# Expert weights read as contiguous row groups, with the rows they meet in a permuted column order

## The chip, the cores and the metric

The kernel runs on one core of a Trainium2 chip. The metric is device time in microseconds (us) of one execution, lower is better. The core has a matrix engine (TensorE, PE in the profile, with its weight loads as PEld), a vector engine (VectorE, DVE), a scalar engine (ScalarE, ACT), GpSimd (POOL) and SyncE (SP), which issues most of the transfers (DMA) from HBM, the memory of the chip, to SBUF, the memory beside the engines. PSUM is the memory that matmuls write, in eight banks.

## The reference, cut to what matters

One layer of an encoder for two groups of tokens (256 prompt tokens and 64 sample tokens, 320 in all). After retention, attention and a first layer norm, its last part is a mixture of 32 experts, of which each token uses two:

```python
h = x * (1 + sc2) + sh2                              # 320 x 1024
logits = h @ w_rg + b_rg, h @ w_re + b_re            # router: 4 groups, 32 experts
# for each expert e, the tokens t that chose it, with gate g:
a, u = jnp.split(h[t] @ w_e_in[e], 2, axis=-1)       # w_e_in[e]: 1024 x 1024
y    = ((jax.nn.silu(a) * u) @ w_e_out[e]) * g       # w_e_out[e]: 512 x 1024
x = layer_norm(alpha * x + (1 + g2) * y_moe)
```

All is in float32. A sum over the 1024 columns of `h` (or the 512 of `silu(a) * u`) may be taken in any order, as long as the rows of the weight go in the same order.

## The kernel before, in words

The instructions of each engine are written out by hand, in one program for each engine, with semaphores between them. Every weight passes through the same stream in pieces of 1 MB (128 partitions x 2048 float32): SyncE loads a piece into one of six buffers `w_raw`; ScalarE rounds it to the reduced float format of fast matmuls (`w_hi`, three buffers, L816 and L973); VectorE takes the difference `w_lo = w_raw - w_hi` (L1061, L1566); TensorE multiplies by both. So the product keeps nearly full precision.

The dense part of the layer takes the first 680 us or so. Then `h2`, the input of the experts, is made on VectorE for three tiles of up to 128 tokens (L1417, L1419, L1421), turned by TensorE (L1925) and copied to `h2T` (L961) for the router (L1914), and written to HBM (L726, L728). VectorE works out from the router's logits which tokens each expert has. An *item* is one expert with up to 64 of its tokens; in this input there are 32 items.

For item e, GpSimd gathers the rows of `h2` from HBM into `x_item` (L741), TensorE turns them in eight blocks of 128 columns (L1957), and ScalarE and VectorE split them (L978, L1570) into `xT_item`. The six pieces of an item in the stream are four of `w_e_in` (j = 0 to 3, two blocks of 128 rows each) and two of `w_e_out` of the item before (j = 4 and 5). Pieces 0 to 4 are split into `w_hi` and `w_lo`; piece 5 is multiplied as it is, at full precision (L1976). The hidden row `silu(a) * u` of 512 columns is made on VectorE by `hidden` (L1579), turned in four blocks by TensorE (L1983), split (L990, L1583) and met with `w_e_out`. The item's result is added up on VectorE (L1590) and scattered to HBM by GpSimd (L747, L774).

The order of one turn of the loop over the items, which is what the prediction follows:

```python
# VectorE, turn e                        # ScalarE, turn e
item_lo(e, 0)                            item_hi(e, 0)
hidden(e - 1)          # L1579           silu(e - 1)
item_lo(e, 1)                            item_hi(e, 1)
y_sum(e - 2, third)                      y_low(e - 2, ...)
item_lo(e, 2)                            item_hi(e, 2)
hidden_low(e - 1)                        hidden_high(e - 1)
item_lo(e, 3); item_lo(e, 4)             item_hi(e, 3); item_hi(e, 4)
au_sum(e); x_low(e + 1)                  au_low(sub(e, 3)); x_high(e + 1)
```

TensorE, turn e: products of pieces 0 and 1 (for each, four matmuls with `w_hi`, L1964, and four with `w_lo`, L1968), the turning of the hidden rows of item e - 1 (L1983), products of pieces 2 and 3, the turning of the input rows of item e + 1 (L1957), the product of piece 4, and that of piece 5 (L1976). SyncE issues piece j of the next item when `w_lo` j has been made (for piece 5, when its product is done), in the order j = 0 to 5 (L532).

Of the kernel before, what the change touches and what calls it, by code (L numbers as in the profile page):

```python
# [13 lines left out]
ALU = mybir.AluOpType  # L14
# [7 lines left out]
P = 128  # L22
KD = D // P
RH, DK, DV = 4, 128, 256
FH, DH = 16, 64
NG, EG, NE = 4, 8, 32
# [77 lines left out]
def build_layer(nc, i, o, scratch):  # L104
# [26 lines left out]
    def at(name, shape, dt, offset):  # L131
        size = int(np.prod(shape[1:])) * (2 if dt == BF16 else 4)
        assert PH + offset + size <= END, (name, PH, offset, size)
        return nc.alloc_sbuf_tensor_at(name, shape, dt, offset=PH + offset)
# [81 lines left out]
    g1x = at("affine_tmp", [P, D], F32, 16384)  # L216
# [4 lines left out]
    def rt(name, shape, dt=F32):  # L221
        t = at(name, shape, dt, ro["n"])
        ro["n"] += (int(np.prod(shape[1:])) * (2 if dt == BF16 else 4) + 31) // 32 * 32
        assert ro["n"] <= 32768
        return t

    wr = rt("w_router", [P, KD, NG + NE])
# [54 lines left out]
    auS = at("au_sum", [SLOTS, 2, FE], F32, 12288)  # L282
    aA = at("a_silu", [SLOTS, FE], F32, 16384)
    hid = at("hidden", [SLOTS, FE], F32, 18432)
# [13 lines left out]
    def sem(name):  # L298
        return ctx.enter_context(nc.semaphore(name))
# [23 lines left out]
    res_in, ln_in, ln_var, ln_std, h2_ready, h2_out, h2T_done = (  # L323
        sem(n) for n in ("res_in", "ln_in", "ln_var", "ln_std", "h2_ready", "h2_out", "h2T_done"))
    m2_in, m2_ready, wr_in, r_dve, r_act, msk_done, slots_ready, slt_done, idx_ready = (
        sem(n) for n in ("m2_in", "m2_ready", "wr_in", "r_dve", "r_act", "mask_done",
                         "slots_ready", "slt_done", "idx_ready"))
    nb_ready, xn_ready = sem("shift_ready"), sem("normalised")
    row_cp, x_norm, x1_ready, nit_ready = sem("row_copied"), sem("x_normalised"), sem("x1_ready"), sem("items_counted")
    idx_cp, x_landed, x_trans, x_hi, x_split, au_lo, au_drained, silu_ok, hid_ok = (  # L330
        sem(n) for n in ("idx_copied", "x_landed", "x_transposed", "x_hi", "x_split", "au_low_copied",
                         "au_drained", "silu_done", "hidden_done"))
# [48 lines left out]
    def spare(after):  # L381

        return tuple(dense_banks(CI[after] + 1)) + (6, 7)
# [23 lines left out]
    for h in range(RH):  # L407
        s = spare("ga0")
# [42 lines left out]
    def bcast(ap1d, rows):  # L451

        return ap1d.partition_broadcast(rows)

    w_in_e = i["w_e_in"][0].rearrange("e (k p) n -> e p k n", p=P)
    w_out_e = i["w_e_out"][0].rearrange("e (k p) n -> e p k n", p=P)
    E0 = N0 + 4
    assert E0 % NRAW == 0 and E0 % NSPL == 0
    PLAIN = 5
# [108 lines left out]
    def _(pool):  # L568
        st = Steps(pool, own_pool)
# [56 lines left out]
        for t in range(3):  # L626
            rows = P if t < 2 else DEC
# [23 lines left out]
        for t in range(3):  # L651
            rows = P if t < 2 else DEC
            st(nc.gpsimd.tensor_scalar(qaug[0:rows, t, :, DH], f_tok[0:rows, q_slots[t], :], 8.0, None, ALU.mult))
        for t in range(4):
            rows = P if t < 3 else DEC
# [60 lines left out]
            st.settle()  # L716

        pool.wait_ge(evacuated, CI["wo0"] + 1)
        pool.dma_start(wr[:, :, 0:NG], i["w_rg"][0].rearrange("(k p) n -> p k n", p=P)).then_inc(wr_in, 16)
        pool.dma_start(wr[:, :, NG:], i["w_re"][0].rearrange("(k p) n -> p k n", p=P)).then_inc(wr_in, 16)  # L720
        pool.dma_start(br[:, 0:NG], bcast(i["b_rg"][0], P)).then_inc(wr_in, 16)
        pool.dma_start(br[:, NG:], bcast(i["b_re"][0], P)).then_inc(wr_in, 16)

# [64 lines left out]
        for t in range(3):  # L788
            rows = P if t < 2 else DEC
# [18 lines left out]
    def _(act):  # L808
# [13 lines left out]
        def copy_bank(key, dst, src):  # L822

            b, _, f, d = use[key]
            act.wait_ge(*f)
            st(nc.scalar.activation(dst, src(b), ACT.Copy), d)
# [8 lines left out]
        def split_hi(kind, dst):  # L835
            for k in range(KD):
                b, _, f, _ = use[(kind, k)]
                act.wait_ge(*f)
                st(nc.scalar.activation(dst[:, k, 0:T], b[:, 0:T], ACT.Copy), ts_hi)

        act.wait_ge(c_in, 32)
        st(nc.scalar.activation(cs2[:], c2[:], ACT.Silu), c_silu)
        b, _, f, _ = use["cT"]
        act.wait_ge(*f)
        act.wait_ge(fills_done, 1)
# [208 lines left out]
    def _(dve):  # L1054
        st = Steps(dve, own_dve)
        V = nc.vector
# [226 lines left out]
        for t in range(3):  # L1283
            rows = P if t < 2 else DEC
# [4 lines left out]
        for t in range(3):  # L1289
            rows = P if t < 2 else DEC  # L1290
# [11 lines left out]
        for t in range(3):  # L1302
            rows = P if t < 2 else DEC
# [9 lines left out]
        for w_, op in ((gnw, ALU.mult), (gnb, ALU.add)):  # L1313
            st.settle()
            for t in range(3):
                rows = P if t < 2 else DEC
# [3 lines left out]
        for t in range(3):  # L1320
            rows = P if t < 2 else DEC
# [91 lines left out]
        for t in range(3):  # L1413
            rows = P if t < 2 else DEC
            xt, ht = x1[0:rows, t, :], h2[0:rows, t, :]
            m2 = m2p if t < 2 else m2s
            st(V.tensor_scalar(xt, xt, mv[0:rows, t, 0:1], mv[0:rows, t, 1:2], ALU.subtract, ALU.mult), x_norm)  # L1417
            st.settle()
            st(V.tensor_tensor(ht, xt, m2[0:rows, 1, :], ALU.mult))  # L1419
            st.settle()  # L1420
            st(V.tensor_tensor(ht, ht, m2[0:rows, 0, :], ALU.add), h2_ready)  # L1421


        iota = const("iota")
# [151 lines left out]

        def hidden(e):
            dve.wait_ge(silu_ok, e + 1)
            V.tensor_tensor(hid[:], aA[:], auS[:, 1, :], ALU.mult).then_inc(hid_ok, 1)  # L1579

        def hidden_low(e):
            dve.wait_ge(hh_hi, e + 1)
# [14 lines left out]
        def item_steps(e, second, third):  # L1597
            item_lo(e, 0)
            hidden(e - 1)
            item_lo(e, 1)  # L1600
            if second:
                y_sum(e - 2, third)
            item_lo(e, 2)
            hidden_low(e - 1)
            item_lo(e, 3)
            item_lo(e, 4)
            au_sum(e)
            x_low(e + 1)
# [4 lines left out]
        with dve.Fori(3, n_items) as e:  # L1613
            item_steps(e, True, True)
        item_lo(n_items, 0)
        hidden(n_items - 1)
        item_lo(n_items, 1)
        y_sum(n_items - 2, True)
# [426 lines left out]
```

## Time and profile before

| what | value |
|---|---|
| median of 3 runs | 1299.65 us (1297.51 to 1302.85) |
| the profiled execution | 1297.03 us, span from first to last instruction 1295.2 us |
| TensorE busy | 1104.2 us, 85% |
| VectorE busy | 894.2 us, 69% |
| ScalarE busy | 634.2 us, 49% |
| HBM read | 299.97 MB |
| expert loads | 128 pieces of `w_e_in` and 64 of `w_e_out`, 1 MB each |

The busy shares are averages over stages that differ. The loop over the items runs from about 725 us to 1245 us of the span, 40% of it; in it all of TensorE, VectorE and the transfer engines are marked busy for nine tenths of the time or more.

### The profile page before, as it was taken

To read this page: it belongs to the slowest core of one execution; us is meant where nothing else is said; L and a number is where in the kernel's file an instruction comes from. 1 tells how busy PE (TensorE), PEld (TensorE's weight loads), DVE (VectorE), ACT (ScalarE), POOL (GpSimd) and SP (SyncE) were. 2 spreads that over 40 slices of the span, in tenths; PEclk is the share of its full clock that TensorE was granted. 3 is DMA by queue.
4 is the path that set the end of the run, shared out by engine and by line. 5 is a ranking of instruction groups with operands and counts; after the bars stand their busy time and mean duration, and the time that the engine had idled before them with its cause. 6 is when DMAs were issued, how large, how long until landed. Compare 5 with 4: busy or idle time off the path is not lost.

```text
span 1295.2 us, 13399 instructions
## 1 busy us (share of the span) xinstructions
PE 1104.2 (85%) x4460; PEld 761.4 (59%) x4460; DVE 894.2 (69%) x974; ACT 634.2 (49%) x639; POOL 267.6 (21%) x227
## 2 busy tenths in 40 slices
PE   5798899888899999999854799999999999999960
PEld 2365568566687666678644556666666666666640
DVE  3868843367464333345596699999999999999957
ACT  3654232222322222332221477777777777777732
POOL 0331940010001000000460741111111111111210
PEclk8798989988999555589785699999999999999985
DMA  9767243153725500024623589999999999999933
GB/s 321 253 238 257 94 152 130 48 169 104 272 73 137 205 0 0 0 98 162 213 68 109 190 336 389 389 393 393 395 395 393 397 391 396 394 390 400 397 110 116
DMA packets 102661, 303.33 MB, mean 234 GB/s; under 512 B 10740, under 2 KB 10788, under 8 KB 102118
## 3 DMA queue, kind: packets, MB, share of 16 engines
q1 hardware_dynamic: 92888, 282.75, 58.6%
q0 software_dynamic: 9744, 20.19, 5.2%
q8 instruction: 18, 0.29, 0.1%
q14 instruction: 11, 0.09, 0.0%
HBM read 299.97 MB, written 14.73 MB: 243 GB/s over the span
## 4 chain that ended last, share of the span: by engine, by line
PE 59%; DVE 18%; DMA 7%; ACT 7%; issue 5%; POOL 4%; SPq 0%; ACTq 0%; POOLq 0%; DVEq 0%
PE banks L1968 9%; PE banks L1976 7%; PE banks L1964 7%; PE banks L1694 6%; PE banks L1700 6%; DVE w_lo L1566 6%; ACT w_hi L973 5%; PE banks L1696 4%; DMA w_raw<-in_w_in 3%; DVE w_lo L1061 3%; PE banks L1727 2%; PE banks L1957 2%; ACT w_hi L816 2%; PE banks L1983 1%; DMA w_raw<-in_w_ada 1%
## 5 line engine op out<-in xcount | busy, mean ns | idle before, releaser
L1566 DVE TENSOR_TENSOR w_lo<-w_raw,w_hi 128x2048 fp32r<-128x2048 f32 x157 | 361.3, 2318 | 36.8 <-ACT w_hi L973 36.8
L973 ACT ACTIVATE w_hi<-w_raw 128x2048 fp32r<-128x2048 f32 x157 | 295.5, 1903 | 0.2 <-issue 0.2
L1061 DVE TENSOR_TENSOR w_lo<-w_raw,w_hi 128x2048 fp32r<-128x2048 f32 x72 | 173.2, 2423 | 137.8 <-ACT w_hi L816 137.7
L816 ACT ACTIVATE w_hi<-w_raw 128x2048 fp32r<-128x2048 f32 x72 | 136.5, 1910 | 210.5 <-PE banks L1700 94.7
L1968 PE MATMUL banks<-w_lo,xT_item 128*128 128x512 f32 x512 | 150.5, 416 | 45.2 <-DVE w_lo L1566 45.2
L1964 PE MATMUL banks<-w_hi,xT_item 128*128 128x512 f32 x512 | 158.9, 433 | 4.2 <-ACT w_hi L973 2.8
L1694 PE MATMUL banks<-w_hi,h_hi 128*128 128x512 f32 x384 | 142.2, 411 | 13.1 <-ACT w_hi L816 12.6
L1968 PEld LDWEIGHTS banks<-w_lo,xT_item 128*128 128x128 f32 x512 | 93.5, 193 | 91.3 <-DVE w_lo L1566 73.1
L1964 PEld LDWEIGHTS banks<-w_hi,xT_item 128*128 128x128 f32 x512 | 96.0, 193 | 39.1 <-issue 14.3
L1976 PE MATMUL banks<-w_raw,hiddenT 128*128 128x512 f32 x248 | 111.4, 592 | 0.0
L1700 PE MATMUL banks<-w_lo,h_hi 128*128 128x512 f32 x384 | 108.2, 404 | 2.4 <-DVE w_lo L1061 2.4
L747 POOL DMA_INDIRECT scratch_y<-y_item,slot_row x29 | 62.8, 2166 | 229.2 <-DVE y_item L1590 212.5
L1696 PE MATMUL banks<-w_hi,h_lo 128*128 128x512 f32 x256 | 105.2, 411 | 0.0
L1694 PEld LDWEIGHTS banks<-w_hi,h_hi 128*128 128x128 f32 x384 | 75.1, 196 | 34.0 <-ACT w_hi L816 14.9
L1700 PEld LDWEIGHTS banks<-w_lo,h_hi 128*128 128x128 f32 x384 | 73.6, 193 | 22.3 <-DVE w_lo L1061 4.6
L1976 PEld LDWEIGHTS banks<-w_raw,hiddenT 128*128 128x128 f32 x248 | 47.0, 189 | 47.3 <-issue 44.5
L741 POOL DMA_INDIRECT x_item<-scratch_h,slot_token x32 | 32.3, 1009 | 183.1 <-PE banks L1957 153.9
L994 ACT ACTIVATE au_low<-banks 64x1024 f32<-64x1024 f32 x32 | 32.8, 1024 | 62.2 <-PE banks L1968 62.2
L1696 PEld LDWEIGHTS banks<-w_hi,h_lo 128*128 128x128 f32 x256 | 50.9, 199 | 11.9
L1717 PE MATMUL banks<-w_lo,c_parts 128*64 128x512 f32 x96 | 34.1, 488 | 15.6 <-DVE w_lo L1061 15.2
L986 ACT ACTIVATE y_low<-banks 64x1024 f32<-64x1024 f32 x32 | 32.8, 1024 | 26.4 <-PE banks L1976 17.3
L1575 DVE TENSOR_TENSOR au_sum<-banks,au_low 64x1024 f32<-64x1024 f32 x32 | 38.9, 1216 | 7.7 <-ACT au_low L994 5.2
(438 smaller groups left out, 1579.3 us busy)
## 6 DMA issues: line engine op xcount, KB each, us to landing
w_raw<-in_w_e_in SPq DMA_DIRECT2D x128, 1024.0 KB, 7.3
w_raw<-in_w_e_out SPq DMA_DIRECT2D x64, 1024.0 KB, 6.0
w_raw<-in_w_in SPq DMA_DIRECT2D x32, 1024.0 KB, 9.0
w_raw<-in_w_ada SPq DMA_DIRECT2D x24, 1024.0 KB, 7.2
bias_rows<-in_b_in SPq DMA_DIRECT2D x16, 256.0 KB, 4.8
w_raw<-in_w_ret_proj SPq DMA_DIRECT2D x4, 1024.0 KB, 17.2
w_raw<-in_w_fox_proj SPq DMA_DIRECT2D x4, 1024.0 KB, 18.8
w_raw<-in_w_o SPq DMA_DIRECT2D x4, 1024.0 KB, 5.1
```

Of the source, the lines that this page charges most:

```text
L747: nc.gpsimd.indirect_dma_start(yd[:, :], bass.IndirectOffsetOnAxis(ap=row[:, e:e + 1], axis=0), ySb[:].rearrange("p a b -> p (a b)"), None ...
L816: nc.scalar.activation(whi[n % NSPL][:], raw[n % NRAW][:], ACT.Copy).then_inc(hi_done, 1)
L973: nc.scalar.activation(whi[ss][:], raw[j][:], ACT.Copy).then_inc(hi_done, 1)
L1061: V.tensor_tensor(wlo[n % NSPL][:], raw[n % NRAW][:], whi[n % NSPL][:].bitcast(F32), ALU.subtract).then_inc(lo_done, 1)
L1566: V.tensor_tensor(wlo[ss][:], raw[j][:], whi[ss][:].bitcast(F32), ALU.subtract).then_inc(lo_done, 1)
L1575: V.tensor_tensor(auS[:], banks[0:SLOTS, 0:2, :], auLo[:], ALU.add).then_inc(au_drained, 1)
L1694: mm(b[:, :], H[:, k, cols], whi[n % NSPL][:, kk, :], start=(k == 0), stop=False)
L1696: mm(b[:, :], L[:, k, cols], whi[n % NSPL][:, kk, :], start=False, stop=False)
L1700: last = mm(b[:, :], H[:, 4 * s + kk, cols], wlo[n % NSPL][:, kk, :], start=False, stop=(s == 1 and kk == 3))
L1964: mm(bank[b0 + half], X[:, k0 + kk, :], whi[ss][:, 2 * kk + half, :], start=(first and kk == 0), stop=False)
L1968: last = mm(bank[b0 + half], X[:, k0 + kk, :], wlo[ss][:, 2 * kk + half, :], start=False, stop=(final and kk == 1))
L1976: last = mm(bank[b0 + half], X[:, k0 + kk, :].bitcast(F32), raw[rs][:, 2 * kk + half, :], start=False, stop=(kk == 1))
```

## The change

`w_e_in`, `w_e_out` and the two router weights are read with another order of their rows. Before, partition p of block k held row 128 k + p, so that a piece of two blocks took two separate runs of 4 KB for each partition. After, partition p of block k holds row 8 p + k (for `w_e_out`, 4 p + k), so that a piece of two blocks is one run of 8 KB for each partition. The columns of `h2` and of the hidden row are put into the same order when they are written: position 128 k + p holds column 8 p + k (4 p + k). The last VectorE operation of `h2` and the operation `hidden` do that by reading their inputs with a stride: 8 elements (32 bytes) in `h2`, 4 elements (16 bytes) in `hidden`; both write neighbouring elements. The first product of `h2` goes to the buffer `affine_tmp` instead of `h2`, since the second can't permute in place. All turnings on TensorE read 128 neighbouring columns, as they did.

```diff
-    w_in_e = i["w_e_in"][0].rearrange("e (k p) n -> e p k n", p=P)
-    w_out_e = i["w_e_out"][0].rearrange("e (k p) n -> e p k n", p=P)
+    w_in_e = i["w_e_in"][0].rearrange("e (p k) n -> e p k n", p=P)
+    w_out_e = i["w_e_out"][0].rearrange("e (p k) n -> e p k n", p=P)
...
-        pool.dma_start(wr[:, :, 0:NG], i["w_rg"][0].rearrange("(k p) n -> p k n", p=P)).then_inc(wr_in, 16)
-        pool.dma_start(wr[:, :, NG:], i["w_re"][0].rearrange("(k p) n -> p k n", p=P)).then_inc(wr_in, 16)
+        pool.dma_start(wr[:, :, 0:NG], i["w_rg"][0].rearrange("(p k) n -> p k n", p=P)).then_inc(wr_in, 16)
+        pool.dma_start(wr[:, :, NG:], i["w_re"][0].rearrange("(p k) n -> p k n", p=P)).then_inc(wr_in, 16)
...
-            st(V.tensor_tensor(ht, xt, m2[0:rows, 1, :], ALU.mult))
-            st.settle()
-            st(V.tensor_tensor(ht, ht, m2[0:rows, 0, :], ALU.add), h2_ready)
+            st(V.tensor_tensor(g1x[0:rows, :], xt, m2[0:rows, 1, :], ALU.mult))
+            st.settle()
+            st(V.tensor_tensor(ht.rearrange("r (k p) -> r k p", k=KD), g1x[0:rows, :].rearrange("r (p k) -> r k p", k=KD),
+                               m2[0:rows, 0, :].rearrange("r (p k) -> r k p", k=KD), ALU.add), h2_ready)
...
-            V.tensor_tensor(hid[:], aA[:], auS[:, 1, :], ALU.mult).then_inc(hid_ok, 1)
+            V.tensor_tensor(hid[:].rearrange("s (k p) -> s k p", k=4), aA[:].rearrange("s (p k) -> s k p", k=4),
+                            auS[:, 1, :].rearrange("s (p k) -> s k p", k=4), ALU.mult).then_inc(hid_ok, 1)
```

## Rows read from the trace of the kernel before

**Rows 1.** One turn by windows: us; PE, PEld, DVE, ACT, POOL; clock, transfer share, GB/s.

```profile
913.57:929.95 16.38, 15.02 (x63) 9.92 (x63) 15.07 (x11) 12.55 (x11) 2.96 (x2) 1.00 1.02 395
```

**Rows 2.** Transfers from 760 to 1200 us: one queue, then issues by line.

```profile
q1 hardware_dynamic: 43807, 168.88, 98.7%
...
w_raw<-in_w_e_in SPq DMA_DIRECT2D x107, 1024.0 KB, 7.3
```

**Rows 3.** Waits from 760 to 1200 us: total us, times, longest.

```profile
PEld banks L1968 <- DVE w_lo L1566: 58.9, 53, 1.5
...
DVE w_lo L1566 <- ACT w_hi L973: 31.3, 54, 0.6
```

**Rows 4.** Waits of SyncE's queue, 700 to 1200 us.

```profile
SPq L532 <- DVE w_lo L1566: 232.3, 114, 8.6
SPq L532 <- PE banks L1976: 131.8, 28, 4.7
```

**Rows 5.** The tile w_raw from 760 to 1200 us: time from issue to landing.

```profile
DMA to landing us min/median/max: 4.8/7.3/9.1
```

**Rows 6.** Timeline of one turn: start, duration, instruction, idle before.

```profile
914.22 2.29 DVE L1566 TENSOR_TENSOR w_lo<-w_raw,w_hi 128x2048 fp32r<-128x2048 f32 x1 [0.61 <-ACT w_hi L973]
...
916.43 0.68 DVE L1579 TENSOR_TENSOR hidden<-a_silu,au_sum 64x512 f32<-64x512 f32 x1
...
917.03 2.28 DVE L1566 TENSOR_TENSOR w_lo<-w_raw,w_hi 128x2048 fp32r<-128x2048 f32 x1
...
918.09 8.27 SPq L532 DMA_DIRECT2D w_raw<-in_w_e_in  x4
...
919.40 0.89 PEld L1968 LDWEIGHTS banks<-w_lo,xT_item 128*128 128x128 f32 x4
...
925.88 0.77 PEld L1968 LDWEIGHTS banks<-w_lo,xT_item 128*128 128x128 f32 x4 [1.50 <-DVE w_lo L1566]
...
928.66 1.91 ACT L973 ACTIVATE w_hi<-w_raw 128x2048 fp32r<-128x2048 f32 x1
```

**Rows 7.** The chain that ended last, one turn: start, us, what.

```profile
937.11 0.56 PE banks L1983 x5
...
937.97 1.92 ACT w_hi L973
...
939.91 2.30 DVE w_lo L1566
...
942.26 1.20 PE banks L1968 x4
```

**Rows 8.** VectorE groups by shape, 600 to 735 us: busy, mean ns.

```profile
L1419 DVE TENSOR_TENSOR h<-x,mod_prompt 128x1024 f32<-128x1024 f32 x2 | 2.4, 1224 | 0.1
...
L1505 DVE TENSOR_REDUCE choice_pos<-onehot_tmp 128x6 f32<-128x192 f32 x1 | 0.4, 353 | 0.0
...
L1456 DVE TENSOR_REDUCE expert_logits<-expert_masked 128x24 f32<-128x96 f32 x1 | 0.3, 316 | 0.0
...
L1496 DVE TENSOR_REDUCE extra_items<-count_cmp 128x32 f32<-128x128 f32 x1 | 0.3, 286 | 0.0
```

**Rows 9.** Timeline where the third tile of h2 is turned.

```profile
680.42 1.22 DVE L1421 TENSOR_TENSOR h<-h,mod_sample 64x1024 f32<-64x1024 f32 x1
```

**Rows 10.** The chain that ended last, 670 to 735 us.

```profile
677.20 1.24 DVE h L1421
...
678.48 1.97 PE banks L1925 x8
...
683.71 1.04 PE banks L1925 x8
...
730.07 2.78 DVE hidden L1579
```

**Rows 11.** Page, groups: an operation that every item has once.

```profile
L1575 DVE TENSOR_TENSOR au_sum<-banks,au_low 64x1024 f32<-64x1024 f32 x32 | 38.9, 1216 | 7.7 <-ACT au_low L994 5.2
```

**Rows 12.** Transfer rate in 40 slices of 0 to 100 us (2 KB runs).

```profile
GB/s 14 299 324 388 421 245 288 386 388 385 388 387 244 352 406 114 389 383 317 381 281 206 213 0 38 228 281 368 401 360 395 320 227 203 217 22 2 14 297 362
```

## The prediction

> **What bounds the kernel now.** The change touches the item loop and the `h2` step ahead of it, so I read those stages alone. First the windows: one turn of the loop takes 16.38 us, and in it TensorE is busy 15.02 us, VectorE 15.07 us and the transfer engines all the time, at 395 GB/s [rows 1]. Three candidates look full, and the transfers look fullest: their queue holds the engines for 98.7% of the stretch from 760 to 1200 us [rows 2]. If they set the pace, longer runs might pay.
>
> So next the waits, which tell who is late. In that stretch TensorE waits for `w_lo` and VectorE for `w_hi` [rows 3]; no line of that view has an engine waiting for `w_raw`. The queue waits instead: in 700 to 1200 us SyncE stood 232.3 us for `w_lo` and 131.8 us for the product of piece 5, that is for a buffer to come free [rows 4]. A transfer lands 7.3 us after issue, at most 9.1 [rows 5]. How much time has it? Piece 0 is issued at 918.09 and ScalarE wants it at 928.66 [rows 6]: 10.6 us. The transfers are busy, but early by 1.5 us at worst and 3.3 us at the median. They don't set the pace.
>
> What does is read from the chain that ended last [rows 7]: turning of the hidden rows, `w_hi` of piece 3, `w_lo` of piece 3, its product. Ahead of the turning stand only products of TensorE. But the timeline shows a second cycle of the same length beside it [rows 6]. VectorE does `w_lo` 0 at 914.22, `hidden` at 916.43, `w_lo` 1 at 917.03 without a gap, and ends that at 919.31; TensorE loads its first weights for the product of `w_lo` 1 at 919.40. That is 0.09 us later, and where TensorE surely waited for `w_lo` (the 1.50 us ahead of 925.88 [rows 6]) the chain shows 0.04 to 0.05 us from the end of `w_lo` to the load: 2.30 us from 939.91 ends at 942.21, the product is at 942.26 [rows 7]. So `w_lo` 1 comes with at most 0.05 us to spare. Whatever delays it delays the turning, then `w_hi` 3, `w_lo` 3, the product, `au_low`, `w_hi` 0 and the next `w_lo` 0: a closed cycle.
>
> **The change part by part.**
>
> *Longer runs.* They are worth nothing while transfers aren't waited for. In the first 100 us, with runs of 2 KB, the queue sustained 385 to 388 GB/s in a row of slices [rows 12], with 4 KB runs 395 [rows 1]: even the rate seems to depend little on the run. I take 0. What hides it is the 1.5 to 3.3 us above. The cost if the new addresses are slower instead: 6 pieces of 1.05 MB make 6.29 MB in 16.38 us, or 384 GB/s for the weights alone; below about that rate the loop waits for them.
>
> *Router weights.* Two small GpSimd loads, of the same pieces of 16 and 128 bytes at the destination, so I take the same cost: nothing, as no engine waits for them in the chain [rows 10].
>
> *First product into `affine_tmp`.* It is the same shape, 1.224 us [rows 8], and GpSimd's last use of that buffer is waited for already: 0.
>
> *Strided reads.* This is the part that costs. No `tensor_tensor` of the trace reads with such a stride, but one reduction does: L1456 reads 96 elements, each 32 bytes from the one before within its group of four. It took 316 ns. Reductions with neighbouring elements took 353 ns for 192 elements and 286 ns for 128 [rows 8], so 1.05 ns an element over a base of 152 ns; 96 elements should take 253 ns. The stride cost 63 ns, 0.66 ns for each element.
>
> The bounds from this: below, 0 (if those 63 ns are peculiar to the reduction). The row's rate gives `hidden` 512 x 0.66 = 0.34 us. If an element takes two cycles instead of one, which a short row may not show in full, the extra is one more 1.05 ns: 0.54 us. If each of the two strided inputs pays at the row's rate, 0.68 us. I take the middle of the row's rate and the doubling, 0.44 us, so `hidden` 0.68 to 1.12 us: the row is the only one near, but it is short and has one input, where these have two, so I lean up from it. For `h2`, 1024 elements: 0.68, 1.07, 1.35 us; I take 0.87.
>
> The Trainium skill has a rule that speaks against this change: Advanced Engine Details and Errata, SBUF Cachelines, says that SBUF is read by lines of 16 bytes and that an access pattern with another line for each access pays a penalty, with no figure. Both new strides (16 and 32 bytes) are of that kind, and the row agrees in sign.
>
> *What of it is on the path.* `hidden` is called once an item, 32 times [rows 11], right ahead of `w_lo` 1. Its extra less the 0.05 us to spare goes through the cycle each time; in the first turn `hidden` stands in the chain itself [rows 10], and at the end the last `y_item` stands behind it on VectorE. So 32 x (0.44 - 0.03) = 13.1 us, with 0.03 as a middle for what is spare. Queued behind `hidden` on VectorE are `w_lo` 1, `y_item`, `w_lo` 2 and the low half of `hiddenT`; all move by the same amount, and so do the transfers that wait for them. The transfers get more time, so they are still not late.
>
> `h2`: the second operation of tiles 0 and 1 is in the chain (1.24 us at 677.20, then TensorE's turning at 678.48 [rows 10]). The third tile is ready at 680.42 + 1.22 = 681.64 [rows 9], but TensorE turns it at 683.71 [rows 10], so its own extra 0.87 lies under those 2 us. 2 x 0.87 = 1.7 us.
>
> Sum: 13.1 + 1.7 = 14.8 us. The profiled execution, 1297.03 us, becomes 1311.9; it lies 2.6 us below the median of the runs, 1299.65. The forecast is for the median: **1314 us**.
>
> **The rivals.**
>
> *Strides are free.* The 63 ns belong to the reduction. Then `hidden` stays 0.68 us, nothing on the path changes, and the time is 1299.65 us, no change. For it: a single short row. Against it: the other reductions fit one line to the nanosecond or two, this one is 25% off. The Trainium skill has a rule that would give this: VectorE: DVE Perf Modes, Mode 1× (REGULAR), says that the base mode yields one result a cycle and names odd strides among what it takes. The trace does not bear it out where L1456 is concerned. Chance 0.2. To it I add the case that the loop has more give than I read, so that only part of `hidden` shows and the whole stays under 6.5 us: 0.03.
>
> *The transfers were the bound after all.* Both look full [rows 1, 2]. If longer runs sped them, the turn could shrink towards VectorE's 15.07 us of work: 31 turns x 1.3 = 40 us, down to 1259 us. It needs transfers that are waited for, and no such wait is there [rows 3]; it would begin to count only if the waits ascribed to `w_hi` were in truth waits for `w_raw`. Chance 0.04.
>
> *The new addresses are slower.* Partitions now start 32 KB apart in `w_e_in` and 16 KB in `w_e_out`, instead of 4 KB. The point from which it decides is a landing later than 10.6 us after issue, or a rate below 6.29 MB / 16.8 us = 374 GB/s. At 324 GB/s, a slice of [rows 12], a turn would take 19.4 us and the time would be 1299.65 + 31 x 3.0 = 1393 us. Nothing in the trace speaks for it. Chance 0.04.
>
> **How the numbers follow.** The forecast case (strides cost, the loop passes it on) has 0.69. Its own range runs from the row's rate, 32 x (0.34 - 0.05) + 1.4 = 10.7, so 1310 us, to both inputs paying, 32 x (0.68 - 0.01) + 2.7 = 24.1, so 1324 us. To leave out no more than 0.2 in all, the range must take in free strides too, with the scatter of runs: 1298 to 1325. What a measurement here can tell from no change is about 0.5%, 6.5 us. Faster is the second rival with a little for scatter, 0.05; the same is the first, 0.22; slower is the forecast and the last rival, 0.73.
>
> **What would show it.** In the profile after: `hidden` (L1579 before) at 1.0 to 1.2 us and never below 0.9; the second operation of `h2` at about 2.1 us, the first at 1.22 still; turns of the item loop of 16.8 us; waits of TensorE for `w_lo` 1 that were not there, with all other idle times as before; landing times no longer than 7.3 us; half as many packets for the experts if a packet is a run. It is wrong if `hidden` stays at 0.68 us, if the turn is longer while `hidden` isn't, if it is longer by less than `hidden` is, or if a wait for `w_raw` turns up.

## The result and the profile after

| | before | after |
|---|---|---|
| median | 1299.7 us (13 runs, 1297.51 to 1305.01) | 1307.59 us (13 runs, 1301.54 to 1310.71) |
| profiled execution | 1297.03 us | 1303.19 us |
| span | 1295.2 us | 1301.3 us |
| one turn of the item loop, median | 16.38 us | 16.60 us |
| `hidden`, median | 0.68 us | 1.07 us |

The changed kernel takes 1.0048 of the time before, with an interval of 1.0031 to 1.0065. That is 6.2 us (4.0 to 8.4), which is also the difference of the means of the runs; the medians lie 7.9 us apart. So it is slower, by about the 0.5% that the prediction called no change. The forecast was 1314 us, 14 us above the median before. The direction is right, the size is about half.

Everything behind the making of `h2` has moved down by one or two lines: `hidden` is now L1580, `w_lo` L1567, the products are L1966 (`w_hi`), L1970 (`w_lo`) and L1978 (plain), the turning of the hidden rows L1985.

The first row sums up `hidden`, which now reads with a stride: count, then the shortest, median and longest duration in ns, then the first and the last start.

```profile
L1580 DVE TENSOR_TENSOR hidden<-a_silu,au_sum x32: 1052/1068/3325, 727.5 to 1249.8; 64x512 f32<-64x512 f32 x32
```

And from the timeline of `h2`'s making:

```profile
671.08 2.00 DVE L1421 TENSOR_TENSOR h<-affine_tmp,mod_prompt 128x1024 f32<-128x1024 f32 x1
```

`hidden` took 0.68 us [rows 6] and takes 1.07; the other took 1.22 [rows 8] and takes 2.00. That is (1068 - 676) / 512 = 0.77 ns for each element at steps of 16 bytes, where 676 ns is the median of `hidden` in the runs with neighbouring reads, and (2000 - 1224) / 1024 = 0.76 ns at steps of 32 bytes. The short reduction from which the prediction took its rate gave 0.66 [rows 8]. By the rule of the Trainium skill (Advanced Engine Details and Errata, SBUF Cachelines) there is a penalty for a new line at each access; the trace agrees, and the price is the same for 16 and 32 bytes.

Next the windows, two turns of the loop after the change (columns as in [rows 1]):

```profile
914.95:931.53 16.58, 15.23 (x63) 9.85 (x63) 15.45 (x11) 12.54 (x11) 2.96 (x2) 1.00 0.98 388
931.53:948.15 16.62, 15.28 (x63) 9.87 (x63) 15.47 (x11) 12.57 (x11) 3.15 (x2) 1.00 1.01 396
```

The granted clock is 1.00 in both, so the higher of the two levels, as before. VectorE's work has grown by 0.39 us a turn (15.07 to 15.46), the turn by only 0.22 (16.38 to 16.60). Over 32 items 0.22 us make 7.0 us, which with 2 x 0.78 = 1.6 us for `h2` is 8.6. That is a little more than the ratio gives (4.0 to 8.4 us) and than the medians do.

The two profiled executions show it more sharply, though they lie only 6.2 us apart. First `h2`'s first product, after and before, and then `hidden` of the kernel before:

```profile
669.82 1.22 DVE L1419 TENSOR_TENSOR affine_tmp<-x,mod_prompt 128x1024 f32<-128x1024 f32 x1
```

```profile
672.70 1.22 DVE L1419 TENSOR_TENSOR h<-x,mod_prompt 128x1024 f32<-128x1024 f32 x1
...
L1579 DVE TENSOR_TENSOR hidden<-a_silu,au_sum x32: 675/677/2858, 730.0 to 1244.0; 64x512 f32<-64x512 f32 x32
```

The changed kernel comes to this product 2.9 us sooner, though nothing ahead of it differs but the order of the rows in two small router loads: single executions scatter by as much in their first half. From there to the last `hidden` it takes 1249.8 - 669.82 = 580.0 us, where it was 1244.0 - 672.70 = 571.3: 8.7 us more, as the account has it. (One turn of this execution, the first, is 20.4 us long in place of 16.4, with a granted clock of 0.92; but the loop also begins earlier, and the second product of a piece 5 stands at 765.55 us where it stood at 765.98.)

Where the other 0.17 us went is seen in the timeline of one turn:

```profile
917.80 1.07 DVE L1580 TENSOR_TENSOR hidden<-a_silu,au_sum 64x512 f32<-64x512 f32 x1
...
918.80 2.27 DVE L1567 TENSOR_TENSOR w_lo<-w_raw,w_hi 128x2048 fp32r<-128x2048 f32 x1
...
919.84 0.89 PEld L1966 LDWEIGHTS banks<-w_hi,xT_item 128*128 128x128 f32 x4
920.07 1.10 PE L1966 MATMUL banks<-w_hi,xT_item 128*128 128x512 f32 x4
...
921.12 0.76 PEld L1970 LDWEIGHTS banks<-w_lo,xT_item 128*128 128x128 f32 x4 [0.40 <-DVE w_lo L1567]
921.13 1.20 PE L1970 MATMUL banks<-w_lo,xT_item 128*128 128x512 f32 x4
...
922.25 0.48 PEld L1985 LDWEIGHTS banks<-pack,hidden 64*128 64x128 f32 x5 [0.37 <-issue]
922.25 0.62 PE L1985 MATMUL banks<-pack,hidden 64*128 64x64 f32 x5
```

The weight load for `w_lo` 1 now waits 0.40 us, as forecast in kind. But there is no idle time on the row of its matmuls. While nothing is late, the matmuls run 0.23 us behind their loads (919.84 and 920.07). When the load is late they run right with it (921.12 and 921.13). So the loads run ahead, and a late one first uses that up. Part of it is lost again, since the four matmuls then take 1.20 us in place of 1.10. From this load to the turning of the hidden rows it is now 1.13 us (921.12 to 922.25). The same stretch before, in the timeline of the kernel before:

```profile
919.63 1.10 PE L1968 MATMUL banks<-w_lo,xT_item 128*128 128x512 f32 x4
...
920.66 0.48 PEld L1983 LDWEIGHTS banks<-pack,hidden 64*128 64x128 f32 x5 [0.37 <-issue]
```

With the load at 919.40 [rows 6] it was 1.26 us. Now the account closes: `hidden` is 0.39 us longer, 0.04 us of that was to spare before the load (the prediction's step), 0.13 us are made up between load and turning, and 0.22 us are left.

No line of the waits from 760 to 1200 us has an engine waiting for `w_raw`; one that was not there before is TensorE's for `x_item`, once, 1.7 us. TensorE's waits for `w_lo` grew from 53 to 79 (of 27 turns, so one more a turn), 9.6 us in all:

```profile
PEld banks L1970 <- DVE w_lo L1567: 68.5, 79, 1.3
...
DVE w_lo L1567 <- ACT w_hi L973: 27.7, 54, 1.2
```

And the transfers of that stretch:

```profile
q1 hardware_dynamic: 22763, 165.78, 95.2%
...
w_raw<-in_w_e_in SPq DMA_DIRECT2D x105, 1024.0 KB, 6.9
```

About half as many packets, a share of 95.2% in place of 98.7%, and landing 6.9 us after issue in place of 7.3 [rows 2]. For each percent of the engines' time the queue moved 165.78 / 95.2 = 1.741 MB, against 168.88 / 98.7 = 1.711 before: 1.8% more. Longer runs do make the transfers cheaper, and nobody was waiting for them.

### The profile page after: what moved, and what is told of

It reads as the page before. It is cut to its first block, busy times and chain, and to the rows that moved or that the text cites. A ratio compares the mean times of both kernels' runs of the same rounds, so it can differ in the third digit from the quotient of the medians.

```text
span 1301.3 us, 13399 instructions
## 1 busy us (share of the span) xinstructions
PE 1105.5 (85%) x4460; PEld 756.1 (58%) x4460; DVE 906.7 (70%) x974; ACT 634.4 (49%) x639; POOL 277.5 (21%) x227
## 4 chain that ended last, share of the span: by engine, by line
PE 60%; DVE 14%; DMA 8%; POOL 7%; ACT 6%; issue 4%; SPq 1%; ACTq 0%; POOLq 0%; DVEq 0%
PE banks L1970 9%; PE banks L1978 7%; PE banks L1966 7%; PE banks L1696 7%; PE banks L1702 6%; DVE w_lo L1567 5%; PE banks L1698 4%; ACT w_hi L973 4%; DMA w_raw<-in_w_in 3%; DVE w_lo L1061 2%; PE banks L1959 2%; PE banks L1729 2%; ACT w_hi L816 1%; PE banks L1985 1%; DMA w_raw<-in_w_ada 1%
## 5 line engine op out<-in xcount | busy, mean ns | idle before, releaser
L1567 DVE TENSOR_TENSOR w_lo<-w_raw,w_hi 128x2048 fp32r<-128x2048 f32 x157 | 360.3, 2312 | 32.7 <-ACT w_hi L973 32.7
L973 ACT ACTIVATE w_hi<-w_raw 128x2048 fp32r<-128x2048 f32 x157 | 295.6, 1903 | 0.2 <-issue 0.2
L1970 PE MATMUL banks<-w_lo,xT_item 128*128 128x512 f32 x512 | 152.5, 420 | 45.6 <-DVE w_lo L1567 45.6
L1966 PE MATMUL banks<-w_hi,xT_item 128*128 128x512 f32 x512 | 159.1, 433 | 4.2 <-ACT w_hi L973 2.8
L1970 PEld LDWEIGHTS banks<-w_lo,xT_item 128*128 128x128 f32 x512 | 91.1, 192 | 100.6 <-DVE w_lo L1567 85.3
L1966 PEld LDWEIGHTS banks<-w_hi,xT_item 128*128 128x128 f32 x512 | 95.9, 193 | 39.0 <-issue 14.1
L1978 PE MATMUL banks<-w_raw,hiddenT 128*128 128x512 f32 x248 | 111.5, 592 | 0.0
L1978 PEld LDWEIGHTS banks<-w_raw,hiddenT 128*128 128x128 f32 x248 | 47.0, 190 | 47.2 <-issue 44.5
L741 POOL DMA_INDIRECT x_item<-scratch_h,slot_token x32 | 36.7, 1146 | 174.8 <-PE banks L1959 146.6
L994 ACT ACTIVATE au_low<-banks 64x1024 f32<-64x1024 f32 x32 | 32.8, 1024 | 60.1 <-PE banks L1970 60.1
L1592 DVE TENSOR_TENSOR y_item<-banks,y_low 64x1024 f32<-64x1024 f32 x32 | 38.8, 1213 | 8.0 <-ACT y_low L986 8.0
```

The source lines that it names most:

```text
L973: nc.scalar.activation(whi[ss][:], raw[j][:], ACT.Copy).then_inc(hi_done, 1)
L1567: V.tensor_tensor(wlo[ss][:], raw[j][:], whi[ss][:].bitcast(F32), ALU.subtract).then_inc(lo_done, 1)
L1592: V.tensor_tensor(ySb[:], banks[0:SLOTS, 2:4, :], yLo[:], ALU.add).then_inc(y_drained, 1)
L1966: mm(bank[b0 + half], X[:, k0 + kk, :], whi[ss][:, 2 * kk + half, :], start=(first and kk == 0), stop=False)
L1970: last = mm(bank[b0 + half], X[:, k0 + kk, :], wlo[ss][:, 2 * kk + half, :], start=False, stop=(final and kk == 1))
L1978: last = mm(bank[b0 + half], X[:, k0 + kk, :].bitcast(F32), raw[rs][:, 2 * kk + half, :], start=False, stop=(kk == 1))
```

## The experiments

Eleven kernels, each set against runs of the kernel before that were made with it. The turn is that of the profiled execution, the median of 30 turns between successive plain products of the item loop; single turns that are longer are named in the text. Where a part of the row order is left out, the text says so. For the three reordered kernels, whose turns vary, it is the mean of 28 turns between successive `hidden`, without the first two and the last.

| kernel | median us | ratio to before | turn us |
|---|---|---|---|
| runs alone | 1301.29 | 1.0015 [0.9998, 1.0031] | 16.38 |
| `hidden` alone | 1303.70 | 1.0038 [1.0023, 1.0053] | 16.60 |
| `h2` alone | 1302.44 | 1.0024 [1.0009, 1.0040] | 16.37 |
| after, `hidden` behind `w_lo` 1 | 1297.24 | 0.9986 [0.9972, 0.9999] | 16.37 |
| strided writes | 1303.18 | 1.0026 [1.0008, 1.0044] | 16.52 |
| strided turnings | 1335.12 | 1.0281 [1.0248, 1.0314] | 17.35 |
| 0.15 us more behind `hidden` | 1301.05, one run | | 16.37 |
| 0.38 us more behind `hidden` | 1304.54, one run | | 16.55 |
| after, loop reordered | 1283.53 | 0.9875 [0.9852, 0.9897] | 15.94 |
| before, loop reordered | 1290.27 | 0.9918 [0.9899, 0.9936] | 16.21 |
| runs alone, loop reordered | 1282.65 | 0.9859 [0.9837, 0.9881] | 15.90 |

### Longer runs alone

```diff
-    w_in_e = i["w_e_in"][0].rearrange("e (k p) n -> e p k n", p=P)
-    w_out_e = i["w_e_out"][0].rearrange("e (k p) n -> e p k n", p=P)
+    w_in_e = i["w_e_in"][0].rearrange("e (p k) n -> e p k n", p=P)
+    w_out_e = i["w_e_out"][0].rearrange("e (p k) n -> e p k n", p=P)
```

The permutation of `h2`, of the hidden row and of the router weights is left out; the work of each engine is that of before.

> The weights of the experts are read in 8 KB runs, but no column is permuted (the router's weights, h2 and hidden stay as before), so hidden rows and weight rows don't match: the kernel leaves the permutation out, and its work is otherwise that of the kernel before. Theory A (transfers are early, the loop is paced by the engines): turns of the item loop stay at 16.38 us, the time is that of before within 3 us, landing times about 6.9 us. Rival B (8 KB runs give something that the strided reads hid): turns under 16.3 us and a time 3 to 10 us below before. Rival C (the new addresses cost part of the loss): turns of 16.45 us or more, 2 to 7 us slower.

1301.29 us over 12 runs, ratio 1.0015 with an interval that holds 1. Turns of 16.38 us but for one of 17.89. `w_raw` landed at 4.9, 6.9 and 9.1 us (shortest, median, longest), where it was 4.8, 7.3 and 9.1 [rows 5]. So in the turns the longer runs bring nothing and the new addresses cost nothing. The loss isn't in the transfers.

### `hidden` alone, and `h2` alone

The first takes the new order for `w_e_out` and the strided `hidden`; the second takes it for `w_e_in` and the router weights, with the strided operation of `h2`. Neither leaves anything out.

```diff
+            V.tensor_tensor(hid[:].rearrange("s (k p) -> s k p", k=4), aA[:].rearrange("s (p k) -> s k p", k=4),
+                            auS[:, 1, :].rearrange("s (p k) -> s k p", k=4), ALU.mult).then_inc(hid_ok, 1)
```

> Only w_out_e is read in the new order and only hidden is made with a strided read; h2, the router and w_in_e stay. Theory A (the loss is hidden's extra 0.39 us less about 0.17 us that the loop can absorb, 32 times): hidden 1.07 us, turns of 16.60 us, about 7 us slower than before. Rival B (the recorded step: nothing is absorbed): turns of 16.7 us or more, 11 us slower. Rival C (the loss of the turns is due to the addresses of w_in_e): turns of 16.38 us.

> Only w_in_e, the router's weights and h2 are in the new order; hidden and w_out_e stay as before. Theory A: the second operation of h2 takes 2.00 us, turns stay at 16.38 us, and the time is 1.6 us above before (two tiles of 0.78 us), which is hardly told from no change. Rival C (addresses of w_in_e): turns above 16.45 us and 4 us or more slower.

With `hidden` alone: 1303.70 us, 1.0038 (3.0 to 6.9 us more), and turns of 16.60 us, those of the whole change. In the turns this is 32 x 0.22 = 7.0 us; the totals show a little less. `hidden` took 1.07 us. TensorE's loads waited for `w_lo` 80 times, 70.2 us, as after the whole change:

```profile
PEld banks L1969 <- DVE w_lo L1566: 70.2, 80, 1.3
```

With `h2` alone: 1302.44 us, 1.0024, and turns of 16.37 us, those of before, but for three of about 17.9. `h2`'s two strided operations stand in the chain at 1.99 and 2.01 us:

```profile
672.89 1.99 DVE h L1421
...
676.90 2.01 DVE h L1421
678.91 0.04 issue
678.95 1.97 PE banks L1926 x8
```

So 2 x 0.77 = 1.5 us come from here. The three long turns are something else: the window of one of them shows a granted clock of 0.92 in place of 1.00, so part of it at the lower level, after TensorE had been busy 16.65 of 18 us in the window before, as much as in the window of the dip.

```profile
880.00:898.00 18.00, 16.65 (x65) 11.16 (x64) 16.09 (x13) 14.19 (x12) 3.45 (x3) 0.92 0.99 396
862.00:880.00 18.00, 16.65 (x72) 11.22 (x71) 16.56 (x12) 14.16 (x13) 3.42 (x3) 1.00 1.00 393
```

Each such dip costs about 1.5 us, and their number differs from execution to execution. That is one source of the scatter of single times, and why the turn is the better measure here than the total. The two parts add to 0.62%, the whole is 0.48%; with intervals of 0.15% each way they agree.

### `hidden` behind `w_lo` 1

The changed kernel with one step moved. If the loss of the turns comes from `w_lo` 1 being late and not from VectorE's work as such, it must vanish though `hidden` stays as long.

```diff
             item_lo(e, 0)
-            hidden(e - 1)
             item_lo(e, 1)
+            hidden(e - 1)
```

> The changed kernel, with hidden moved behind w_lo 1 on VectorE; TensorE wants the hidden rows only after the product of w_lo 1, which takes 1.1 to 1.2 us. Theory A (the cost is the delay of w_lo 1): TensorE no longer waits for w_lo 1, the turns go back to about 16.38 us though hidden still takes 1.07 us, and 6 to 7 us of the loss come back. Rival B (VectorE's total work paces the loop, so the order doesn't matter): turns stay at 16.60 us. Rival D (hidden 1.07 us and the w_lo 1 product 1.2 us are so close that the turning of the hidden rows waits instead): turns of 16.4 to 16.5 us.

1297.24 us, 0.9986, and turns of 16.37 us. `hidden` takes 1.085 us in the median. The whole loss of the turns is gone, so the place is shown: the wait of TensorE for `w_lo` 1. (The total even lies 0.1 to 3.6 us under that of before, though `h2`'s 1.5 us are still in it. The turns don't show where these few us come from, and they were not traced.) From the timeline of this kernel, `hidden` ends at 921.75 and TensorE turns its rows at 922.59, when the products that stand ahead are done:

```profile
920.67 1.08 DVE L1580 TENSOR_TENSOR hidden<-a_silu,au_sum 64x512 f32<-64x512 f32 x1
...
921.34 0.89 PEld L1970 LDWEIGHTS banks<-w_lo,xT_item 128*128 128x128 f32 x4
...
922.59 0.48 PEld L1985 LDWEIGHTS banks<-pack,hidden 64*128 64x128 f32 x5 [0.37 <-issue]
...
922.82 2.27 DVE L1567 TENSOR_TENSOR w_lo<-w_raw,w_hi 128x2048 fp32r<-128x2048 f32 x1
```

The last row is `w_lo` 2. It starts 0.23 us after the turning; before the change it started 0.29 us ahead of it (920.37 and 920.66), after the change 0.12 us (922.13 and 922.25). So what stands behind `hidden` on VectorE, `y_item` and `w_lo` 2, is as late here as after the change and more, and costs nothing: `w_lo` 1 alone is the place.

The run also shows where the next limit is: `w_lo` 1 now has plenty to spare, but the turn is no shorter than before. The other closed cycle (turning, `w_hi` 3, `w_lo` 3, its product) holds 16.37 us by itself, as the prediction's "second cycle of the same length beside it" had it.

### Doses of delay

The kernel before, with a memset on VectorE right behind `hidden`, of columns that nobody reads then: 108 columns of a scratch tile, or 384 (the first and the second added line; each kernel has one of them). They measure how much of a delay the loop passes on, without strides.

```diff
             V.tensor_tensor(hid[:], aA[:], auS[:, 1, :], ALU.mult).then_inc(hid_ok, 1)
+            V.memset(oht[:].rearrange("p t c n -> p (t c n)")[:, 0:108], 0.0)
+            V.memset(yg[:, 0, 0, 0:384], 0.0)
```

> The kernel before, with a memset of 108 columns right behind hidden on VectorE, about 0.15 us of additional work at the same place as the strides' 0.39 us. Theory A (0.17 us of a delay of w_lo 1 are absorbed): turns stay at 16.38 us. Rival, the recorded step (at most 0.05 us to spare): turns of 16.48 us.

> The same with a memset of 384 columns, about 0.38 us. Theory A: turns of 16.38 + 0.38 - 0.17 = 16.59 us, as with the strided read, so that nothing but the added time of VectorE is at work. Rival, the recorded step: 16.71 us. Rival, the stride does something beside its duration: less than 16.5 us.

The small dose, from its timeline:

```profile
920.71 0.68 DVE L1579 TENSOR_TENSOR hidden<-a_silu,au_sum 64x512 f32<-64x512 f32 x1
...
921.35 0.15 DVE L1580 MEMSET onehot_tmp<- 128x108 f32 x1
921.43 2.22 DVE L1566 TENSOR_TENSOR w_lo<-w_raw,w_hi 128x2048 fp32r<-128x2048 f32 x1
...
923.70 0.86 PEld L1969 LDWEIGHTS banks<-w_lo,xT_item 128*128 128x128 f32 x4
```

`w_lo` 1 starts 0.72 us after `hidden`, where it was 0.60 [rows 6]. But it takes 2.22 us here in place of 2.28, and what counts is its end: 2.94 us after the start of `hidden`, where it was 2.88, so only 0.06 us later. Its load comes 0.02 us later (2.99 in place of 2.97), its matmuls no later, and the turn is 16.37 us. That is no test between the two theories, since by the prediction's step too only 0.01 us would have gone through. The large dose:

```profile
920.26 0.68 DVE L1579 TENSOR_TENSOR hidden<-a_silu,au_sum 64x512 f32<-64x512 f32 x1
...
921.27 2.22 DVE L1566 TENSOR_TENSOR w_lo<-w_raw,w_hi 128x2048 fp32r<-128x2048 f32 x1
...
923.54 0.76 PEld L1969 LDWEIGHTS banks<-w_lo,xT_item 128*128 128x128 f32 x4 [0.37 <-DVE w_lo L1566]
```

`w_lo` 1 starts 1.01 us after `hidden`, again takes 2.22 us, and ends 3.23 us after the start of `hidden`, 0.35 later than before. The load waits 0.37 us and the turn is 0.17 us longer (16.55): 0.18 us of the delay are taken. By the same measure the strided `hidden` of the change makes the end of `w_lo` 1 0.39 us late (3.27 us after the start of `hidden`, from 917.80, 918.80 and 2.27) for 0.22 us a turn: 0.17 us are taken. So plain work delays the loop just as the stride's extra does, and 0.17 us is what the rows give: 0.05 us ahead of the load, and the 0.22 us by which the matmuls catch up with it (0.23 to 0.01 behind), less the 0.10 us by which they then take longer. Both doses are single runs, so what they say rests on the turns, of which each execution has some thirty, and not on the totals. Why `w_lo` 1 takes 0.06 us less in both is not known.

### Strided writes, and strided turnings

Two other ways to the same column order. In the first VectorE reads neighbours and writes with a stride of 512 bytes, in `hidden` and in `h2`. In the second VectorE's operations are those of before, and TensorE's weight loads of the three turnings read `h2`, `x_item` and `hidden` with the stride.

```diff
+            V.tensor_tensor(hid[:].rearrange("s (k p) -> s p k", k=4), aA[:].rearrange("s (p k) -> s p k", k=4), ...
```

```diff
-                last = step(bank[5][:, SLOTS * k:SLOTS * k + SLOTS], hid[:, P * k:P * k + P], ident[0:SLOTS, 0:SLOTS])
+                last = step(bank[5][:, SLOTS * k:SLOTS * k + SLOTS], hid[:].rearrange("r (p k) -> r k p", k=4)[:, k, :], ident[0:SLOTS, 0:SLOTS])
```

> The changed kernel, but hidden and the second operation of h2 read neighbouring elements and write with a stride (512 bytes between one element and the next, of 4 or 8). Theory A (the price is one of reading with a stride): hidden back to 0.68 us, h2 to 1.22 us, turns of 16.38 us, time within 2 us of before. Rival B (a stride costs the same on the write side): hidden about 1.07 us, turns of 16.60 us, time as the changed kernel, 8 us above before.

> The weights in the new order, h2 and hidden stored as before; the permutation is made where TensorE turns the rows: each block is every eighth column of h2 and x_item, every fourth of hidden (stride 32 and 16 bytes for the weight load of TensorE). Theory A (VectorE's strided read was the whole loss): hidden 0.68 us; if TensorE reads strides freely, turns of 16.38 us and the time of before. Rival B (TensorE's loads pay as VectorE's do, about 1.6 times for the stride): the loads of the turnings go from 0.14 to 0.22 us or more, 12 of them a turn, all on TensorE's path: turns of 16.6 to 17.4 us, 7 to 30 us slower.

Writes cost what reads do. `hidden` and the two tiles of `h2`:

```profile
L1580 DVE TENSOR_TENSOR hidden<-a_silu,au_sum x32: 1031/1064/3291, 730.7 to 1255.2; 64x512 f32<-64x512 f32 x32
...
L1421 DVE TENSOR_TENSOR h<-affine_tmp,mod_prompt x2: 1897/1903/1909, 674.1 to 677.9; 128x1024 f32<-128x1024 f32 x2
```

The ratio, 1.0026 [1.0008, 1.0044], is not told apart from that of the change itself, but the turn is: 16.52 us, 0.08 less. VectorE goes on a little sooner after a strided write:

```profile
908.37 1.07 DVE L1580 TENSOR_TENSOR hidden<-a_silu,au_sum 64x512 f32<-64x512 f32 x1
...
909.28 2.28 DVE L1567 TENSOR_TENSOR w_lo<-w_raw,w_hi 128x2048 fp32r<-128x2048 f32 x1
```

`w_lo` 1 starts 0.91 us after `hidden`, in place of 1.00 after the change, and ends 3.19 us after it: 0.31 us later than before, for 0.14 us a turn. Again 0.17 us are taken. That two strided inputs and one strided output cost the same, 0.39 us for 512 elements, suggests that the two inputs didn't pay one after the other; no run strides one input alone.

With the stride on TensorE the kernel takes 1335.12 us, 1.0281 [1.0248, 1.0314]. The weight loads of the two turnings in the loop, means over 766 to 1200 us:

```profile
L1957 PEld LDWEIGHTS banks<-pack,x_item 64*128 64x128 f32 x216 | 31.3, 245 | 8.7 <-issue 8.7
L1983 PEld LDWEIGHTS banks<-pack,hidden 64*128 64x128 f32 x125 | 22.0, 283 | 9.2 <-issue 9.2
```

In the kernel before these means are 156 and 168 ns. Here the turning takes longer as its loads do, and it stands in the chain:

```profile
906.36 1.37 PE banks L1957 x9
...
916.95 0.96 PE banks L1983 x5
```

The second was 0.56 us [rows 7], and the first 0.80 in the chain after the change: together 0.97 us more a turn, and the turn is 0.97 us longer. The same permutation costs over four times as much there as on VectorE (0.97 us a turn against 0.22, in all 2.81% against 0.48%). In this execution five turns of the thirty are 1.5 us longer still, with dips of the clock as above.

### The loop reordered

The prediction held that the transfers were early, and the runs alone bear that out. Whether the longer runs are ever worth something is a question for a loop that goes faster. Three steps are moved: `hidden` behind `w_lo` 1, the split of the hidden rows (`hidden_high` on ScalarE, `hidden_low` on VectorE) behind piece 3. That breaks both cycles.

```diff
             item_lo(e, 0)
-            hidden(e - 1)
             item_lo(e, 1)
+            hidden(e - 1)
...
             item_lo(e, 2)
-            hidden_low(e - 1)
             item_lo(e, 3)
+            hidden_low(e - 1)
...
             item_hi(e, 2)
-            hidden_high(e - 1)
             item_hi(e, 3)
+            hidden_high(e - 1)
```

It was made of the kernel after, of the kernel before, and of the runs alone (which again leaves the permutation out, and so has no strides).

> The changed kernel with three moves in the item loop: hidden behind w_lo 1 on VectorE, hidden_high behind w_hi 3 on ScalarE, hidden_low behind w_lo 3 on VectorE, so that w_hi 3 and w_lo 3 no longer wait for the turning of the hidden rows. By the engines alone the turn becomes about 15.4 us (VectorE's work is 15.06 + 0.39 = 15.45). Theory T (transfers now bind, and 8 KB runs help): from the queue's share, 95.2% at 16.60 us with 8 KB runs, the transfers need 15.8 us a turn: turns of 15.8 us, waits for w_raw in the profile, about 18 us under before. Theory E (transfers never bind, their share overstates them): turns of 15.4 to 15.5 us, no wait for w_raw, about 28 us under before.

> The kernel before with the same three moves, 4 KB runs. Theory T: 98.7% at 16.38 us means that the transfers need 16.2 us a turn: turns of 16.2 us, waits for w_raw, 5 us under before, and so slower than the same moves with 8 KB runs. Theory E: turns of 15.3 to 15.4 us, about 30 us under before, and faster than with 8 KB runs and strides by the 1.6 us of h2.

> The same moves with 8 KB runs and no permuted columns (hidden and weight rows don't match; the kernel leaves the permutation out), so no strided read. Theory T: turns of 15.8 us, as with the strides, since the transfers bind in both. Theory E: turns of 15.3 to 15.4 us as with 4 KB runs, with VectorE no longer full.

1283.53 us, 1290.27 us and 1282.65 us. The kernel after with this order is the fastest that leaves nothing out: 0.9875 of before, 16 us less. First the windows of the item loop, for the three in that order:

```profile
760.00:1180.00 420.00, 396.62 (x1642) 262.44 (x1641) 405.81 (x266) 332.16 (x264) 209.58 (x54) 1.00 1.00 402
```

```profile
760.00:1180.00 420.00, 393.67 (x1613) 257.41 (x1612) 388.64 (x261) 336.66 (x260) 150.94 (x53) 1.00 1.02 396
```

```profile
760.00:1180.00 420.00, 398.67 (x1643) 263.12 (x1642) 395.35 (x266) 339.98 (x264) 169.69 (x54) 1.00 1.00 402
```

Then the waits for transfers, from 760 to 1200 us. The kernel after, reordered:

```profile
ACT w_hi L973 <- DMA w_raw<-in_w_e_in: 3.8, 8, 1.1
```

The kernel before, reordered:

```profile
ACT w_hi L973 <- DMA w_raw<-in_w_e_in: 31.5, 63, 1.5
```

The runs alone, reordered:

```profile
ACT w_hi L973 <- DMA w_raw<-in_w_e_in: 22.4, 45, 1.5
```

With runs of 4 KB, ScalarE now waits for `w_raw` 63 times, a line that the view of before does not have [rows 3], and `w_raw` lands 11.2 us after issue, past the 10.6 us that the prediction gave it. The rate stands at 396 GB/s, and in the kernel before it already gave 395 [rows 1]. The mean turn of 16.21 us hides two stretches. From the second turn to the seventh it is 15.50 us (below), on pieces that had been loaded ahead, and then the kernel has used up its lead. The plain products of this kernel, the eighth, the ninth and the last:

```profile
858.67 1.02 PE L1976 MATMUL banks<-w_raw,hiddenT 128*128 128x512 f32 x2
...
875.28 1.02 PE L1976 MATMUL banks<-w_raw,hiddenT 128*128 128x512 f32 x2
...
1235.13 0.59 PE L1976 MATMUL banks<-w_raw,hiddenT 128*128 128x512 f32 x1
```

From the ninth to the last are 22 turns of (1235.13 - 875.28) / 22 = 16.36 us. That is what the transfers give with 4 KB runs in this loop, and the turn of before was 16.38. So in the kernel before the transfers had a lead in time, the 1.5 to 3.3 us, but next to none in rate: full and early at once, on the edge of being the bound. The same 22 turns of the runs alone take 16.01 us, of the kernel after 15.95. (The 16.2 us expected from the queue's share are met by 16.21 only because that mean mixes the two stretches.) The gain of 7 to 8 us from longer runs (1290.27 to 1283.53 and 1282.65) is there only in this loop; 22 x 0.35 = 7.7 us.

The strides can be read in the same three kernels. Where neither transfers nor strides bind, in turns 2 to 7 of the kernel before and of the runs alone, the turn is 15.50 us. In the kernel after it is 15.91 nearly throughout, 0.41 more, with VectorE busy 96.6% (405.81 of 420). There VectorE is the bound and the stride is paid whole. The runs alone start at 15.50 and drift to about 16.0 as the transfers fall behind, so that in the total the two differ by 0.9 us and not by 13.

## Why the prediction came out as it did

**What bounds the kernel: right.** That no transfer was waited for, that `w_lo` 1 closes a cycle, and that a second cycle of the same length stands beside it, are all shown: by the runs alone (no change), by `hidden` behind `w_lo` 1 (loss gone, no gain), and by the reordered loop (gain only when both cycles are broken). "The transfers are early" is right of the single transfer; that they had as good as no margin in rate was not seen.

**Longer runs, router weights, the first product: right.** 0 forecast, 1.0015 [0.9998, 1.0031] measured for the runs; the first product of `h2` takes 1.23 to 1.24 us in the chain after.

**The extra of `hidden` and `h2`: right in kind, a little high.** 0.44 us forecast and 0.39 measured; 0.87 and 0.78. The reduction's rate, 0.66 ns, was nearer than the doubling, 1.05; the measured one is 0.77. (The line through the reductions is looser than "to the nanosecond or two": it goes through two sizes, as any line does, and a third, L1518 with 24 elements, took 170 ns where it gives 177. Against 63 ns that matters little.) The third tile of `h2` was hidden, as said: it is ready at 681.15 us and turned at 682.37.

**The failed step is "Its extra less the 0.05 us to spare goes through the cycle each time".** The 0.04 to 0.05 us were read rightly, but they are the slack of the weight load, and what goes on through the cycle is the end of the matmuls. These ran 0.23 us behind their loads, and the stretch from load to turning shrank by 0.13 us when the load was late. So the loop takes 0.17 us of a delay and not 0.03 to 0.05, as the change, the large dose and the strided writes all show. Forecast 32 x 0.41 = 13.1 us, measured 32 x 0.22 = 7.0: of the 6.1 us between, 32 x 0.05 = 1.6 are the extra that was too high, 32 x 0.13 = 4.2 are this, and the rest is 0.04 us to spare where 0.03 was put. The row that would have shown it was in the timeline of before: load at 919.40, its matmul at 919.63. With the measured terms the sum is 1299.7 + 7.0 + 1.6 = 1308.3 us, where 1307.59 was measured. The prediction's own sign of being wrong, a turn that grows by less than `hidden` does, is what came: 0.22 against 0.39 us.

**The rivals.** Free strides: wrong, 0.39 us. "The loop has more give than I read" was the right one in kind, with a chance of 0.03; the total lies at its limit of 6.5 us, a little over by the medians (7.9) and a little under by the ratio (6.2). New addresses slower: wrong, the landing is 6.9 us. Transfers the bound: wrong for this kernel, though nearer than the 1.5 to 3.3 us of slack made it look: once the engines went faster, the transfers gave a turn of 16.36 us with 4 KB runs, where the turn of before was 16.38.

**What stays open.** The 0.17 us stand on delays of 0.31 to 0.39 us; the small dose turned out too small, and nothing between 0.06 and 0.31 us was tried. The few us by which `hidden` behind `w_lo` 1 is under before are not explained. What starts the dips of the granted clock was not tried.

## What to carry to other kernels

When a queue of transfers is full but nobody waits for it, longer runs are worth nothing yet; make the loop faster first and then try them again, since the same edit was worth 7 us once the transfers were late. That transfers land in time shows a lead, not a margin in rate: here the lead lasted six turns. Price a permutation by where it is done: here 0.77 ns for each element on VectorE, in reads or in writes, and over four times the loss when TensorE's weight loads did it; and put it where the engine has slack, not ahead of an operand that a full engine takes at once. To find what a delay costs, measure it at the end of the late operation, and follow it to the end of the matmuls: slack read at the weight load is less than there is.

## What the runs showed of the hardware that was not expected

- VectorE in float32 with two inputs: steps of 16 bytes and of 32 bytes in the reads cost the same for each element (0.77 and 0.76 ns), and steps of 512 bytes in the write cost nearly as much (1064 - 676 = 388 ns for 512, 1903 - 1224 = 679 ns for 1024). The Trainium skill (VectorE: DVE Perf Modes, Mode 1× (REGULAR)) has one result a cycle and counts odd strides among what works; they work, but here a strided operation of 512 elements took 1068 ns in place of 676.
- Weight loads of TensorE read with such a stride take 245 and 283 ns in place of 156 and 168.
- In the reordered loops, which wait for their transfers, 4 KB runs gave 396 GB/s and 8 KB runs 402; in turns, 16.36 and 16.01 us.
- While nothing is late matmuls run 0.23 us behind their weight loads, and a load that comes late makes up 0.13 us of it; with the 0.04 to 0.05 us ahead of the load, 0.17 us of a late operand never reach the turn.
- The granted clock dips for single turns, to 0.92 over 18 us, at about 1.5 us each; the execution of the strided turnings had five such turns, that of `h2` alone three, the others none to two.
